# Cutting a group's weight products into parts, with one piece of side work behind a part, in a two-block transformer kernel

## The reference

```
mod  = c @ w_ada + b_ada                        # six vectors of 2048
h    = rmsnorm(x, g_pre_mix) * (1 + scale1) + shift1
q_a, k_a, v_a, q_h, f_h, i_h, g_h, gate_a, gate_h = split(h @ w_in)
y_a  = sliding_window_attention(rope(q_a), rope(k_a), v_a) @ w_attn_proj
y_h  = (rmsnorm(hgrn2_recurrence(q_h, f_h, i_h)) * sigmoid(g_h)) @ w_hgrn_proj
x    = x + gate1 * rmsnorm((sigmoid(gate_a) * y_a + sigmoid(gate_h) * y_h) @ w_out)
x    = x + gate2 * rmsnorm((silu(g) * u) @ w_ffn_out)     # g, u from the normed x @ w_ffn_in
# second block
y    = concat(chunked_band_attention(...), rmsnorm(gated_linear_attention(...)) * silu(r_g))
x    = x + y @ w_out_2
x    = x + (gelu(conv(g)) * conv(u)) @ w_ffn_down_2
x    = x + sigmoid(rmsnorm(x) @ w_ple_gate_2) * (p_2 @ w_ple_proj_2)
out  = rmsnorm(x, final_norm_w_2)
```

## Time and profile before

| | |
|---|---|
| median of 3 runs | 3098.93 us (3096.09 to 3113.31) |
| the profiled execution | 3098.2 us, of which the span of instructions is 3096.4 us |
| TensorE busy | 2853.6 us, 92% of the span |
| VectorE, ScalarE busy | 1778.2 us (57%), 1273.9 us (41%) |
| `mix_in` from group 4 | 166.15 to 666.75 us |
| `mix_in2` | 1700.47 to 2131.79 us |
| after the last FFN product | 2950.07 to 3096.43 us |

### The profile page before, as it was taken

The page is one execution under the profiler, slowest core; times in us unless marked ns, Lnnn a source line. Parts: engine busy times, 40 slices in busy tenths (PEclk is TensorE's granted clock), DMA queues, the critical chain, the costliest instruction groups (busy, mean ns, idle before and its releaser), DMA issues.

```text
span 3096.4 us, 45327 instructions
## 1 busy us (share of the span) xinstructions
PE 2853.6 (92%) x17746; PEld 2567.6 (83%) x17746; DVE 1778.2 (57%) x1932; ACT 1273.9 (41%) x1445; POOL 232.1 (7%) x163
## 2 busy tenths in 40 slices
PE   4888888889979999999997999989899999999987
PEld 4787776777769998799986998867899988999865
DVE  7865666557874445544466442455476654666444
ACT  2354434333344444333334443443554533444343
POOL 2010020110000010001000000000022110112000
PEclk8998899999989999999998997999999999999999
DMA  9974544458855556655565552334455555555442
GB/s 355 330 245 163 178 157 155 146 183 310 297 191 180 186 190 232 244 181 184 178 242 204 167 187 84 118 127 149 137 176 184 184 188 190 176 189 177 162 167 108
DMA packets 298185, 588.59 MB, mean 190 GB/s; under 512 B 12234, under 2 KB 17342, under 8 KB 296926
## 3 DMA queue, kind: packets, MB, share of 16 engines
q1 hardware_dynamic: 293752, 578.03, 53.8%
q10 hardware_dynamic: 4326, 9.09, 0.8%
HBM read 584.98 MB, written 2.10 MB: 190 GB/s over the span
## 4 chain that ended last, share of the span: by engine, by line
PE 84%; DVE 9%; ACT 3%; issue 2%; DMA 1%; POOL 0%; DVEq 0%; ACTq 0%; POOLq 0%; SPq 0%; PEldq 0%
PE psum L714 13%; PE psum L718 13%; PE psum L716 13%; PE psum L703 13%; PE psum L707 12%; PE psum L705 12%; DVE ada_acc L786 2%; DVE mod_acc L576 2%; DVE w_lo L665 1%; PE bank L842 1%; PE bank L2143 1%; ACT w_hi L653 1%; ACT junk L919 1%; PE bank L1007 0%; DMA gla_gain<-in_gla_norm_w_dram 0%
## 5 line engine op out<-in xcount | busy, mean ns | idle before, releaser
L665 DVE TENSOR_TENSOR w_lo<-raw,w_hi 128x1024 fp32r<-128x1024 f32 x916 | 1176.0, 1296 | 1093.8 <-ACT w_hi L653 1085.6
L653 ACT ACTIVATE w_hi<-raw 128x1024 fp32r<-128x1024 f32 x916 | 953.7, 1047 | 1540.1 <-PE psum L707 761.3
L714 PE MATMUL psum<-h_hi,w_hi 128*128 128x256 f32 x3392 | 963.8, 284 | 1.0 <-PE bank L586 0.7
L716 PE MATMUL psum<-h_lo,w_hi 128*128 128x256 f32 x3392 | 963.1, 284 | 0.0
L718 PE MATMUL psum<-h_hi,w_lo 128*128 128x256 f32 x3392 | 963.0, 284 | 0.0
L714 PEld LDWEIGHTS psum<-h_hi,w_hi 128*128 128x128 f32 x3392 | 653.8, 193 | 2.0 <-issue 1.9
L716 PEld LDWEIGHTS psum<-h_lo,w_hi 128*128 128x128 f32 x3392 | 654.0, 193 | 0.1
L718 PEld LDWEIGHTS psum<-h_hi,w_lo 128*128 128x128 f32 x3392 | 653.8, 193 | 0.0
L703 PE MATMUL psum<-w_hi,h_hi 128*128 128x512 f32 (+1 forms) x992 | 392.3, 395 | 23.0 <-ACT sig_p L1593 7.8
L705 PE MATMUL psum<-w_lo,h_hi 128*128 128x512 f32 (+1 forms) x992 | 388.8, 392 | 0.0
L707 PE MATMUL psum<-w_hi,h_lo 128*128 128x512 f32 (+1 forms) x992 | 388.5, 392 | 0.0
(11 more groups left out here) (315 smaller groups left out, 2028.1 us busy)
## 6 DMA issues: line engine op xcount, KB each, us to landing
raw<-in_w_in_dram SPq DMA_DIRECT2D x120, 1024.0 KB, 5.0
raw<-in_w_ffn_in_dram SPq DMA_DIRECT2D x88, 1024.0 KB, 4.8
raw<-in_w_ffn_up_dram SPq DMA_DIRECT2D x88, 1024.0 KB, 4.8
raw<-in_w_ada_dram SPq DMA_DIRECT2D x64, 1024.0 KB, 5.0
raw<-in_w_ffn_out_dram SPq DMA_DIRECT2D x44, 1024.0 KB, 5.1
raw<-in_w_ffn_down_dram SPq DMA_DIRECT2D x44, 1024.0 KB, 5.1
ada_raw<-in_w_ada_dram SPq DMA_DIRECT2D x64, 512.0 KB, 7.7
raw<-in_w_out_dram SPq DMA_DIRECT2D x32, 1024.0 KB, 5.1
```

The costliest lines, as they stand in the source:

```text
L653: nc.scalar.activation(w_hi[:, slot, :, 0:ncol], raw[:, rs, 2 * h:2 * h + 2, 0:ncol], ACT.Copy).then_inc(split_hi, inc)
L665: nc.vector.tensor_tensor(w_lo[:, slot, :, 0:ncol], raw[:, rs, 2 * h:2 * h + 2, 0:ncol], w_hi[:, slot, :, 0:ncol].bitcast(F32), ALU.subtra ...
L714: pe.matmul(o, fh, hi[:, k, :], start=first and f % 2 == 0, stop=False, skip_group_check=True)
L716: pe.matmul(o, fh, lo[:, k, :], start=False, stop=False, skip_group_check=True)
```

## The change

For each group of `mix_in` and `mix_in2` the new function `parts` gives three parts (3, 3 and 2 halves) or, for groups of 4 halves, two parts (2 and 2). Every engine's stream is now written part by part. Behind a part stands at most one piece of side work, or two small ones, given by the tables `SIDE` and `SIDE_2` (and `SCORES`, `TURN`, `LEVEL_EXP`, and so on, which say the same for each kind). A level's exponent, its factors and its `gram` stand behind different parts. The `mod` units and sums are placed anew (`mod=`), and each sum stands in a later group's part. In the second block the attention result has its own place (`att1_hi`, `att1_lo`), the attention begins two groups sooner, and the gate work of the linear attention stands one to two parts apart. The arena of SBUF begins at a multiple of 128 bytes instead of 32.

At the end, the product of p and `w_ple_proj_2` is a stage `proj` of its own, two units, ahead of the transposes of x; `ple` has four groups that alternate between the PSUM pairs. The squares for the last norm are taken per column block, the final gain is applied per block, and ScalarE and VectorE scale one token tile each, in two halves, with four stores instead of two. The load and the transposes of p are issued earlier.

```diff
-                            mod=[0] * 4 + [2] * 7 + [0, 0, 2, 0, 2, 0, 0, 0, 2, 0])
-        self.mix_gate = Phase(self, D // COLS - 1, [full, half], mod=[2, 2])
+                            mod=[0] * 4 + [2, 2, 2, 1, 1, 2, 2] + [0, 0, 0, 0, 2, 1, 2, 1, 2, 0])
+        self.mix_gate = Phase(self, D // COLS - 1, [full, half], mod=[3, 1])
...
-        self.ple = Phase(self, 1, [full, (PLE // P, COLS)] * (D // COLS))
+        self.proj = Phase(self, 1, [(2 * PLE // P, COLS)] * 2)
+        self.q = [n + 1 for n in self.q]
+        self.ple = Phase(self, 1, [full] * (D // COLS))
...
+    (5, 2): [("attn0_s0", ALL_BANKS)],
+    (6, 0): [("mod_in0", (0, 0, 0, 1))],
+    (6, 1): [("attn0_t0", ALL_BANKS)],
+    (6, 2): [("attn0_s1", ALL_BANKS)],
+    (7, 0): [("attn0_v0", (1, 0, 0, 0))],
...
+LEVEL_EXP = {(10, 2): 0, (11, 0): 1, (11, 2): 2, (12, 1): 3, (13, 0): 4, (14, 0): 5}
+LEVEL_FACTORS = {(10, 2): 0, (11, 1): 1, (12, 0): 2, (13, 0): 3, (13, 1): 4, (14, 1): 5}
+LEVEL_GRAM = {(11, 0): 0, (11, 2): 1, (12, 1): 2, (13, 1): 3, (13, 2): 4, (15, 0): 5}
...
+def parts(phase, g):
+
+    n = phase.end[g] - (phase.end[g - 1] if g else 0)
+    return [(0, 3), (3, 6), (6, 8)] if n == 8 else [(0, 2), (2, 4)]
...
+            if part[0] == 0:
+                pe.wait_ge(psum_free[ph.pair[g]], ph.free(i, g))
+            for idx in range(start + part[0], start + part[1]):
...
+                if part == 1:
+                    pe.wait_ge(sem("p_full"), 16)
+                    transpose_pe(pe, "ple", p_tok, 2)
...
+            for t in range(TT):
+                square_act(act, 6, t, x)
+                proj_act(t)
+            for g in range(2):
+                split_w_hi(act, plan.proj, 0, *span(plan.proj, g))
+                proj_act(2 + g)
```

More of the change, by code:

```diff
@@ L266, in bank_uses @@
             ("ada", (4, 0, 0, 0)), ("first_kv", (0, 1, 0, 0)), ("first_qh", (0, 0, 1, 1))]
[L268 to L282, removed]
-    hooks(0, plan.mix_in, 5)
+    for at in sorted(SIDE):
+        uses += SIDE[at]
     uses += [
@@ L288, in bank_uses @@
         ("norm2", (2, 2, 2, 2))]
-    hooks(1, plan.mix_in2, 6)
+    for at in sorted(SIDE_2):
+        uses += SIDE_2[at]
     return uses + [
@@ L596, in mod_bank, with mod_pe @@
             if name == "mod_in":
-                return f"mod_in{ph.sums[n]}", 0
+                return f"mod_in{n}", 0
             return name, i * len(ph.sums) + n
-        def mod_pe(pe, ph, i, g):
+        def mod_pe(pe, ph, i, g, only=None):
             g0, place_, _ = mod_of(ph)
             for n, due in enumerate(ph.sums):
-                if due != g:
+                if (due != g) if only is None else n != only:
                     continue
@@ L668, in split_w_lo, with span @@
                                             ALU.subtract).then_inc(split_lo, inc)
-        def span(ph, g, final=False):
+        def span(ph, g, final=False, part=None):
             first = (ph.end[g - 1] if g else 0) + 4
             last = ph.end[g] + 4
+            if part is not None:
+                first, last = first + part[0], first + part[1]
             if final:
@@ L679, in products @@
         def products(pe, ph, i, g, hi, lo, k_first=0, transposed=False, ready=None,
-                     hidden=None):
+                     hidden=None, part=None):
             ps = psum[ph.pair[g]]
-            pe.wait_ge(psum_free[ph.pair[g]], ph.free(i, g))
             start, stop = (ph.end[g - 1] if g else 0), ph.end[g]
-            for idx in range(start, stop):
+            part = part or (0, stop - start)
+            if part[0] == 0:
+                pe.wait_ge(psum_free[ph.pair[g]], ph.free(i, g))
+            for idx in range(start + part[0], start + part[1]):
                 _, slot, inc, m, _, _, _, ncol = ph.half(i, idx)
@@ new lines, in _ @@
+                if g > 1:
+                    act.wait_ge(sem("ple_added"), g - 1)
+                nc.scalar.activation(sig_p[:, g % 2], psum[g % 2][:], ACT.Sigmoid).then_inc(psum_free[g % 2], 1)
+                if g:
+                    out_squares_act(g - 1)
+            out_squares_act(3)
+            act.wait_ge(sem("rms"), 8)
+            act.wait_ge(sem("out_gained"), 4)
+            for n in range(2):
+                half = tokbuf[:, 0, n * D // 2:(n + 1) * D // 2]
+                nc.scalar.activation(half, half, ACT.Identity, scale=stats[:, 7, 2:3]).then_inc(sem("result0"), 1)
@@ L1946, in _ @@
+            dve.wait_ge(sem("out_squares"), 2 * (D // COLS))
+            nc.vector.tensor_reduce(stats[:, 7, 0:2], out_sq[:], AX_X, ALU.add).then_inc(sem("squares"), 2)
+            dve.wait_ge(sem("out_gained"), 4)
             dve.wait_ge(sem("rms"), 8)
-            for t in range(TT):
-                nc.vector.scalar_tensor_tensor(tokbuf[:, t, :], x[:, t, :], stats[:, 7, 2 + t:3 + t],
-                                               out_row[:], ALU.mult, ALU.mult).then_inc(sem("result"), 1)
+            for n in range(2):
+                half = tokbuf[:, 1, n * D // 2:(n + 1) * D // 2]
+                nc.vector.tensor_scalar(half, half, stats[:, 7, 3:4], None, ALU.mult).then_inc(sem("result1"), 1)
@@ L2246, in _ @@
             for g in range(len(ph.groups)):
-                products(pe, ph, 0, g, h_hi, h_lo, transposed=g < 4 or g in (6, 7),
-                         ready={0: "norm2", 13: "att1"}.get(g))
-                if 8 <= g < 12:
-                    values_pe(pe, 1, g - 8, pt2, va)
-                if 7 <= g < 11:
-                    turn_pe(pe, 1, g - 7, sm2)
-                if g == 6:
-                    for n in range(6):
-                        pe.wait_ge(psum_free[ph.pair[n]], ph.freed(0, n))
```

894 lines of the change are left out of this document (515 added, 379 removed).

## The result

The changed kernel takes 2956.51 us (median of 4 runs, 2955.91 to 2957.45), beside 3100.68 us for the kernel before in the same comparison (3096.09 to 3113.31). The ratio is 0.953, with a 95% interval of 0.950 to 0.956: 144 us faster. The forecast was 2988 us with a range of 2963 to 3020.

A forecast was written before the change was run, and what follows sets the result against it. TensorE, busy 92% of the span, was taken as the bound, losing time to idle and its lower clock. Savings of 79.3 (`mix_in`), 14.8 (`mix_in2`) and 17.3 us (end) summed to 111.4, giving 2988 us, range 2963 to 3020.

The forecast's parts named there:

- SBUF's new base: Whole kernel: the moved arena changes no instruction's shape and nothing in the rows prices an alignment, so 0 us.
- clock drops that were allowed for: Three drops to the lower clock at 1.7 us in each of `mix_in` and `mix_in2`, 5.1 us added per stage.
- the clock's 14.2 and 10.5 us: `mix_in`: low-clock time removed, 14.2 us from weight products and 10.5 us from side work.
- (14,1): `mix_in`, factors behind a `mod` unit: 9.0 us after the buffer comes free, about 0.8 us of new wait.
- both softmax places: `mix_in`, (5,2) and (8,2), scores ahead of a softmax: 2 us of new wait for both, bounds 0 and 8.
- the keys: `mix_in`, (16,0): VectorE's row takes 7.1 us against 5.5 us of cover, 1.6 us of new wait.
- (10,1): `mix_in2`: one more new wait at this place, 1.0 us.
- (1): Rival: the idle moves; half of `mix_in`'s 66.1 us returns with its clock, 41 us more, 3029 us; chance 0.14.
- (2): Rival: each of 52 breaks in `mix_in` and `mix_in2` lowers the clock, 88 us, 3075 us; chance 0.03.
- (3): Rival: no effect, the waits come again at each piece, 3098 us; chance 0.02.
- (4): Rival: slower, each of `mix_in`'s 32 breaks holds back the splits behind it; 3120 us at 4.7 us each; chance 0.04.
- (5): Rival: better than summed, 17.8 us of new waits and drops do not come, nor `mix_in2`'s small waits; 2966 us; chance 0.09.

The follow-up runs named there:

- `a_off64`: The changed kernel with the arena of SBUF 64 bytes higher: 2974.22 us, 17.7 us slower than the changed kernel.
- `a_off96`: The changed kernel with the arena 96 bytes higher, at the address it had before: 2975.92 us, 19.4 us slower than the changed kernel.
- `b_align128`: The kernel before with the arena alone moved 96 bytes lower, to a multiple of 128 bytes: 3086.72 against 3101.53 us, ratio 0.9942.
- `a_small`: The changed kernel with the product of `qs` one part ahead of the keys' factor and `heads1` one part later: 2953.10 us, 3.4 faster.
- `a_mod_old`: The changed kernel with the `mod` units placed as before, parts and pieces unchanged: 2957.79 us, 1.3 above the changed kernel.
- `a_all64`: The changed kernel with 64 bytes of padding ahead of `h_hi`, so that h, w and the arena move together: 2955.22 us.
- `a_w32`: The changed kernel with 32 bytes of padding ahead of `raw`, `w_hi` and `w_lo`, and the arena 32 bytes higher: 2956.82 us.
- `a_w96`: The changed kernel with 96 bytes of padding ahead of `raw`, `w_hi` and `w_lo`, and the arena 96 bytes higher: 2948.23 us.

## Why the prediction was right, and where it was wrong

**The step that failed** is the sentence on SBUF's new base: it changes no instruction's shape, "so 0". The address is worth 17.7 to 19.4 us in this kernel (`a_off64`, `a_off96`), 18 in the one before (`b_align128`). With the old address the changed kernel takes 2975.9, inside the range and 12 us from the forecast. These 12 us are a second, smaller miss, for the most part clock drops that were allowed for and hardly came (10.2 us in the two stages, of which 1.5 came). It took both: the forecast less the 19.4 us alone would be 2968.6, inside the range as well.

The address effect stood in the trace of before: at the same clock and with the same 512 columns the trace has 22.04 us for 96 products of a group with h or `att`, 229.6 ns each with the start of the group, and 215 products of `hid` in 50 us, 232.6 ns each, in the second FFN, a stretch that the forecast never turned to; from start to start it is 227.1 against 234.3 ns. The forecast's sentence reasoned on splits, which TensorE covers, and never on TensorE's own operands. The Trainium skill, page "TensorE: Matmul & The Clock Gate", section "Step-by-step: what each phase is for", would not have warned of it: by it the next weights come through a read port of their own, and their load takes no SBUF bandwidth from the running matmul. That sentence no run here tests by itself. What the runs show is that the step is not independent of how the two operands lie to each other: 64 bytes between them move it from 120.0 to 115.8 ns. Why, stays open.

**`mix_in`**: mechanism right, 79.3 forecast, 87.3 measured. All removed waits went, the clock's 14.2 and 10.5 us came back. Of the added terms, the waits were 6.2 us against 4.4: 0.8 at (14,1) as forecast, 0 at both softmax places against 2, 1.0 for `w_lo` at an unforeseen place, and 4.4 instead of 1.6 at the keys, where I had left the `mod` unit of 3.2 us out of VectorE's row and priced every split at 1.27 us, also the three that took 3.2 beside GpSimd (2.9 us, see `a_small`). In all of `mix_in` splits slowed in this way cost VectorE 17.4 us more than at 1.22 each, and 5.0 before; TensorE felt it at the keys. The mis-sized terms that make the 8 us are two. One is the clock: three drops at 5.1 in sum, where only the wait ahead of the keys was followed by one (3.0 us at half speed under the keys, 1.5 lost); the waits of 1.0 and 0.8 us were not. The other is the idle: 2.0 net and 4.4 added were forecast, and 1.9 net came, since the 31 breaks overlap more than I had allowed. A small error lies in the 14.2 us that I put down to low clock: 1.4 of it is the step of the 192 products of `rec` (234.2 ns before), the address again.

**`mix_in2`**: 14.8 forecast, 23.6 measured. The wait ahead of `heads1` was forecast at 2.2 and came at 2.9, the one at (10,1) did not come, and none of the three drops did (5.1). In part that is luck: the clock stayed up behind the 2.9 us here, and behind the same wait of 2.9 us it was at 0.50 for 3.4 us in `a_mod_old`, `a_all64`, `a_w32` and `a_w96`. The narrow group still lowers the clock, for 20.5 us instead of 37.5, but under products instead of attention pieces. The rest are small waits of before that the sum had left in place, 2.3 us (a `w_lo` of 1.3, three under 0.5), which went, and up to 2.0 of address.

**The end**: 17.3 forecast, 17.6 measured. Products started 27.0 us in (25.4 forecast), and from the last product 14.4 us were left (12.5 forecast); 87.3 us of products instead of 88.2 and the p transposes' 0.6 instead of 1.3 pay for part of that.

**Elsewhere** nothing was forecast, and 12.6 us came. The address gives 16 to 17; against it stand small losses between the stages, such as 7.1 us instead of 6.0 ahead of the merged transposes.

**The rivals.** (1) The idle does not move: 10.2 us of waits in `mix_in`, all named. (2) Breaks do not lower the clock: 1.00 over `mix_in` with 31 of them. The Trainium skill's page named in the forecast ("TensorE: Matmul & The Clock Gate", section "Part 4: PE-mode transpose") says that transposes do not count as busy for the clock gate. The changed kernel's trace speaks against it, and more plainly than the pieces of before. Ahead of `mix_out` TensorE idles 7.1 us and then does nothing but transposes (L887, 32 of them, from 689.82): the granted clock is 0.50 under the first 27, and 1.00 from 695.5 on, before the first product at 696.03. The keys' transposes, from 477.40, are followed by the same rise at 480.4. (3) and (4) did not come; the price per break that would have turned the sign was 4 us, and `mix_in` holds 6.2 us of new waits in all, 0.2 per break. (5), better than summed, is nearest to what came, at a chance of 0.09: its own mechanism, drops that do not come, gave about 9 us, and the larger part came by one that it did not name. The range was too narrow below because the term at nothing was given no bound of its own where TensorE's operands are concerned.

## What to carry to other kernels

A chain over several engines is hidden by cutting the bound engine's work and putting one cut between each two links; pieces alone, or cuts with the whole chain behind one of them, give much of it back (70 of 87 us, and 47). Before a buffer's move is priced at nothing, count the instructions of the bound engine per unit of time for each pair of operand buffers: equal shapes at unequal steps are an address effect, and a few bytes of padding test it. What delays a piece is the whole row of work on the engine that feeds it, so moving an item within a row without gaps changes nothing; and an item's price is the one it has beside GpSimd's work at that place, not its mean (3.4 us against 1.22 for a split).

## What the runs showed of the hardware

TensorE's step depends on the distance between the SBUF addresses of its stationary and its moving operand, at a granted clock of 1.00 and with the same shapes: 115.8 to 120.0 ns for 256 columns, 226.7 to 234.3 for 512. Shifting both by 64 bytes changed nothing; shifting one gained 40 us in this kernel, and from 226.7 to 234.3 ns it cost 18. The runs cover four distances for one pair of tiles and three for another, and give no rule beyond them. I had expected none of it, and the first account that I formed, by the alignment of one operand, was wrong.

A split on VectorE (128x1024) takes 1.22 us alone and up to 3.43 while a GpSimd instruction runs. The granted clock rises from 0.50 to 1.00 while TensorE does transposes alone (5.7 us of them, behind 7.1 us idle), and it can fall behind a wait of 2.3 to 2.9 us or stay up: behind the same 2.9 us it did either, from one kernel of this study to the next.
